# Attention in a hybrid decoder step: turns ahead of both score blocks in each pair's cycle on TensorE

## The chip, the cores and the metric

The kernel runs on one core of one Trainium2 chip. The metric is the device time of one launch in microseconds (us). The engines are PE (TensorE), DVE (VectorE), ACT (ScalarE), POOL (GpSimd) and SP (SyncE, which only issues transfers here). They run their own queues in order and meet through semaphores.

## The reference

Two layers of a decoder over 1024 prompt tokens and 32 sample tokens (8 sequences of 4), width 1024, in float32. What matters here is the attention of both layers:

```
layer 0:  z = rms_norm(x) @ w_in_a
          q, k, v, xq = split(z)              # 12 query heads, 4 kv heads of 64, 4 memory heads
          o  = softmax with sink of (q.k/8 - slope*dist) over a window of 128 keys, times v
          xo = softmax(xq . mem_k) times mem_v  # 256 memory tokens
          x  = x + concat(o, xo) @ w_out_a
layer 1:  the window part is replaced by a chunked spatial gate; the memory attention stays
both:     x  = x + w_down( silu(causal_dwconv3(h w_g)) * (h w_u) ),  h = rms_norm(x)
```

Queries are taken in blocks of 128; a block sees its own keys and those of the block before.

## The kernel before, in words

Every engine's program is written out by hand, and all waits are on counting semaphores. The projections and the feed-forward part are sequences of "units" on TensorE in which each product is formed from three matmuls of high and low parts (lines 613 to 615); they fill most of the time. Between the input projection and the output projection of each layer stands `prompt_attention(l)`, one function per engine (lines 935, 1361 and 1833; the GpSimd part is the loop at line 570).

The attention of the prompt is cut into items, `item_pairs` (line 124). An item is two heads times one block of 128 queries; two neighbouring blocks b and b+1 make a pair. Layer 0 has 32 pairs: numbers 0 to 7 are memory attention, 8 to 31 window attention, four pairs to each of six head tiles. Of those four the first (pairs 8, 12, 16, ...) has b = 0: its even item sees only 128 keys. Layer 1 has 8 memory pairs. An item n goes through these steps:

- **scores** (`scores(n)`, line 941, matmuls at line 959, tiles of 64x64): TensorE writes two PSUM banks, 2*(n%2) and the next. It may not start before the banks' last reader is done: `ready(n-2)` for a window item, `exped(n-2)` for a memory item.
- **top** (`top(n)`, line 1851): DVE takes the row maximum. For a window item this is one instruction per head that also adds the bias and moves the scores to SBUF (line 1871, and a small copy of the sinks at line 1862 for b < 2); for a memory item one reduction (line 1881). It signals `ready`.
- **exps** (line 1366, recorded at line 1382): ACT, two exponentials with row sums; signals `exped`.
- **scale** (line 1883, recorded at 1885): DVE, a reciprocal of the sums; signals `recip`.
- **norm** (`normalise(n)`, line 547, recorded at 553): POOL multiplies both heads; signals `normed`.
- **turn** (`turn(n)`, line 963, recorded at 975): TensorE transposes the probabilities with matmuls against the identity, tiles of 128x128; waits for `normed(n)`.
- **take** (line 1386, recorded at the helper's line 1180): ACT copies the turned block to SBUF (p_t).
- **values** (`values(n)`, line 979, recorded at 994): TensorE multiplies by the values, tiles of 128x64.
- **out** (line 1887, recorded at 1891): DVE copies a pair's result to z.

The pairs are run as a software pipeline. In cycle `it` of the loop TensorE works on the scores of pair it and on the turns and values of pair it-2; DVE does, in this order, scale(2it-2), out(it-3), top(2it), scale(2it-1), top(2it+1) (lines 1946 to 1956); ACT does take, take, then the exponentials of items 2it and 2it+1 (lines 1424 to 1430); POOL normalises item 2it-2 and 2it-1 as their reciprocals arrive. In what follows "even" and "odd" are the first and the second item of a pair.

Between these cycles stand the steps of the sample tokens' attention (`sample_step`, line 800): one in each of ten cycles, from it = 5 on, in layer 0, and four in layer 1. Their matmuls stand at the end of a cycle on TensorE (lines 808, 836, 841, 850, 855, 876, 883 and 887), their scalings in POOL's queue behind the two norms of a cycle (lines 561 and 566), and their copies on DVE at the end of its cycle (line 1801). POOL also makes the window biases in its spare time (line 544) and clears a buffer (line 579) in its queue after the norms of items 2 and 3.

Of the kernel before, what the change touches and what calls it, by code (L numbers as in the profile page):

```python
# [131 lines left out]
def item(layer, n):  # L132

    kind, q, b = item_pairs(layer)[n // 2]
    return kind, q, b + n % 2
# [21 lines left out]
def step_of(steps, layer, it):  # L157

    return steps[layer].get(it - SAMPLE_AT[layer])


def mem_tile(layer, p):
    return (8 if layer == 0 else 12) + p
# [6 lines left out]
def hybrid_step(nc, d, o, slopes):  # L170
    ctx = ExitStack()
    with ctx:
# [432 lines left out]
        def _(pe):  # L605
# [329 lines left out]
            def prompt_attention(l):  # L935
# [3 lines left out]
                M = len(pairs)  # L939

                def scores(n):
                    kind, q, b = item(l, n)
                    if n >= 2:

                        pe.wait_ge(m["ready"] if item(l, n - 2)[0] == "swa" else m["exped"], n - 1)
                    q0 = TS + b * BLOCK
                    for part in range(2):
                        for half in range(2):
                            rows, lanes = slice(64 * half, 64 * half + 64), slice(64 * part, 64 * part + 64)
                            out = ps[lanes, 2 * (n % 2) + half]  # L950
                            if kind == "swa":

                                w0, w1 = max(BLOCK if b == 0 else 0, 64 * part), 192 + 64 * part
                                keys = z[rows, 6 + q // 3, q0 - BLOCK + w0:q0 - BLOCK + w1]
                            else:
                                w0, w1 = 0, 256
                                keys = mem_k[rows, 2 * l + q, :]
                            tile = q if kind == "swa" else mem_tile(l, q)
                            mm = pe.matmul(out[:, w0:w1], z[rows, tile, q0 + 64 * part:q0 + 64 * part + 64], keys,  # L959
                                           start=True, stop=True)  # L960
                    mm.then_inc(m["scored"], 1)

                def turn(n):
                    kind, q, b = item(l, n)
                    pe.wait_ge(m["normed"], n + 1)
                    if n == 0 and l == 0:
                        pe.wait_ge(m["turned_taken"], 5)
                    if n == 0 and l == 1:
                        pe.wait_ge(m["gate_biased"], NB + 1)
                    if n >= 2:  # L970
                        pe.wait_ge(m["pturned_taken"], n - 1)
                    for kc in range(1 if kind == "swa" and b == 0 else 0, 2):
                        for half in range(2):
                            at = (kc * 2 + half) * P
                            mm = pe.transpose(ps[:, 4 + n % 2, at:at + P], se[:, n % RING, half, kc * P:(kc + 1) * P],  # L975
                                              ident[:, :])
                    mm.then_inc(m["pturned"], 1)

                def values(n):
                    kind, q, b = item(l, n)  # L980
                    pe.wait_ge(m["pturned_taken"], n + 1)
                    if n % 2 == 0 and n >= 2:
                        pe.wait_ge(m["o_taken"], n // 2)
                    kc0 = 1 if kind == "swa" and b == 0 else 0
                    for kc in range(kc0, 2):
                        for half in range(2):
                            if kind == "swa":
                                g = 2 * (q // 3) + half
                                vals = v_tok[:, b - 1 + kc, g * HD:(g + 1) * HD]
                            else:  # L990
                                vals = mem_v[:, l, kc, (2 * q + half) * HD:(2 * q + half + 1) * HD]
                            at = (kc * 2 + half) * P
                            o0 = (n % 2) * P
                            mm = pe.matmul(ps[64 * half:64 * half + 64, 6, o0:o0 + P], vals, pt[:, n % 2, at:at + P],  # L994
                                           start=(kc == kc0), stop=(kc == 1))
                    if n % 2 == 1:
                        mm.then_inc(m["pv"], 1)
# [27 lines left out]
                    gate(lambda: scores(0))  # L1025
                    pe.wait_ge(m["gate_biased"], NB)
                for it in range(0 if l == 1 else 2, M + 2):
                    if it < M and (l == 0 or it > 0):
                        scores(2 * it)
                    if it >= 2:  # L1030
                        turn(2 * (it - 2))
                        turn(2 * (it - 2) + 1)
                    if it < M:
                        scores(2 * it + 1)
                    if it >= 2:
                        values(2 * (it - 2))
                        values(2 * (it - 2) + 1)
                    if l == 0 and it == 2:

                        pe.wait_ge(m["z_normed"], 30)  # L1040
                        for t in range(2):
                            mm = pe.transpose(ps[0:TS, 7, t * P:(t + 1) * P], z[:, 6 + t, 0:TS], ident[:, :])
                        mm.then_inc(m["turned"], 1)
                    sample_step(l, step_of(PE_STEPS, l, it))

            for l in range(2):
# [34 lines left out]
                else:  # L1081
                    first_units(2 * l, s0, r0 // 2)
                    for u in range(2, nu):
# [14 lines left out]
                        if u == len(tiles) + 1:  # L1098
                            mixer_stats(l, m, 2, False, True)
                prompt_attention(l)  # L1100

                s0, r0 = (S_OUTA, R_OUTA) if l == 0 else (S_OUTB, R_OUTB)
# [1230 lines left out]
```

## Time and profile before

| | us |
|---|---|
| median of 3 runs | 2269.54 (2268.39 to 2270.66) |
| the profiled execution, its time | 2269.62 |
| its span | 2267.9 |
| PE busy | 2242.6 (99%) |
| DVE busy | 1129.0 (50%) |
| ACT busy | 662.8 (29%) |
| POOL busy | 552.4 (24%) |
| attention of layer 0, first scores to first product of the output projection | 205.2 to 329.9 |
| attention of layer 1 after its gate, second cycle to the end | 1382 to 1412 |

PE works almost all of the time in the projections and the feed-forward part. The stretch that the change touches is the 125 us of layer 0's attention and the last 30 us of layer 1's. In them a row of the timeline is a start in us, a duration, the engine, the line, the operation, its output and inputs, and in brackets the idle time before it and what ended that. The row of a block of matmuls lasts until the modelled end of the last one, so the next block may start before it ends.

### The profile page before, as it was taken

Reading aid. Unit: us, or ns where it says so; the run is one execution under the profiler, and the core shown is the slowest. Engines: PE = TensorE matmul, PEld = TensorE weight load, DVE = VectorE, ACT = ScalarE, POOL = GpSimd, SP = SyncE. Lnnn points to the kernel's source line nnn. Section 1 sums busy time; section 2 is a strip of 40 time slices with the busy share of each in tenths; the row PEclk is TensorE's granted clock in tenths of the full one; section 3 lists DMA queues with packets and bytes.
Section 4 is the critical chain, followed back from the end, with each engine's and each line's share of the span. In section 5 each row is a group of like instructions: output and inputs, shape, how many; then the busy total and the mean of one; then the engine's idle time right before and its main releaser. Section 6 shows DMA issues by size and latency. Waiting matters only on the chain.

```text
span 2267.9 us, 38768 instructions
## 1 busy us (share of the span) xinstructions
PE 2242.6 (99%) x15074; PEld 2149.9 (95%) x15074; DVE 1129.0 (50%) x2142; ACT 662.8 (29%) x1200; POOL 552.4 (24%) x412
## 2 busy tenths in 40 slices
PE   8999999999999999999999999999999999999999
PEld 7987679999999999999999996999999999999999
DVE  6335681565454554454562236246454555454554
ACT  6313791422211222211253226242221122211121
POOL 0002454322211222211261222332221122211221
PEclk9999999999999999999999999999999999999999
DMA  5223001111111111111111111111110111110112
GB/s 171 84 101 136 21 5 47 38 56 56 46 37 37 46 55 55 37 37 45 47 51 51 47 67 67 38 47 57 56 37 29 54 46 55 51 41 28 46 56 90
DMA packets 39303, 123.39 MB, mean 54 GB/s; under 512 B 5328, under 2 KB 13488, under 8 KB 38416
## 3 DMA queue, kind: packets, MB, share of 16 engines
q1 hardware_dynamic: 36384, 113.25, 15.4%
q10 hardware_dynamic: 2832, 8.94, 1.0%
q8 instruction: 60, 0.98, 0.2%
q14 instruction: 27, 0.22, 0.0%
HBM read 115.57 MB, written 8.63 MB: 55 GB/s over the span
## 4 chain that ended last, share of the span: by engine, by line
PE 94%; DVE 3%; ACT 1%; issue 1%; POOL 0%; DMA 0%; SPq 0%; ACTq 0%; DVEq 0%; POOLq 0%
PE ps L613 29%; PE ps L614 28%; PE ps L615 28%; DVE h_lo L1655 2%; PE ps L959 1%; PE ps L994 1%; PE ps L975 1%; PE ps L808 1%; PE ps L928 1%; ACT s_exp L1382 1%; PE ps L777 0%; PE ps L796 0%; PE ps L931 0%; DMA x<-in_x_t 0%; PE ps L907 0%
## 5 line engine op out<-in xcount | busy, mean ns | idle before, releaser
L613 PE MATMUL ps<-h_hi,w_hi 128*128 128x352 f32 x3120 | 1013.7, 325 | 10.6 <-DVE h_lo L1655 10.0
L614 PE MATMUL ps<-h_lo,w_hi 128*128 128x352 f32 x3120 | 1001.3, 321 | 0.0
L615 PE MATMUL ps<-h_hi,w_lo 128*128 128x352 f32 x3120 | 1000.9, 321 | 0.0
L481 POOL TENSOR_TENSOR w_lo<-raw,w_hi 128x1024 fp32r<-128x1024 f32 x118 | 299.2, 2536 | 1518.2 <-ACT w_hi L1180 1518.2
L613 PEld LDWEIGHTS ps<-h_hi,w_hi 128*128 128x128 f32 x3120 | 586.1, 188 | 31.3 <-issue 20.2
L614 PEld LDWEIGHTS ps<-h_lo,w_hi 128*128 128x128 f32 x3120 | 587.4, 188 | 0.0
L615 PEld LDWEIGHTS ps<-h_hi,w_lo 128*128 128x128 f32 x3120 | 585.8, 188 | 0.0
L2055 DVE TENSOR_TENSOR x<-x,ps 128x352 f32<-128x352 f32 x528 | 270.7, 520 | 170.5 <-PE ps L615 169.7
L613 PE MATMUL ps<-g_hi,d_hi 128*128 128x352 f32 x1056 | 340.2, 322 | 0.0
L614 PE MATMUL ps<-g_lo,d_hi 128*128 128x352 f32 x1056 | 339.9, 322 | 0.0
L615 PE MATMUL ps<-g_hi,d_lo 128*128 128x352 f32 x1056 | 339.7, 322 | 0.0
L1180 ACT ACTIVATE w_hi<-raw 128x1024 fp32r<-128x1024 f32 (+1 forms) x140 | 145.3, 1040 | 417.0 <-PE ps L615 403.2
L615 PEld LDWEIGHTS ps<-g_hi,d_lo 128*128 128x128 f32 x1056 | 198.7, 188 | 0.0
L614 PEld LDWEIGHTS ps<-g_lo,d_hi 128*128 128x128 f32 x1056 | 198.4, 188 | 0.0
L613 PEld LDWEIGHTS ps<-g_hi,d_hi 128*128 128x128 f32 x1056 | 198.3, 188 | 0.0
L1180 ACT ACTIVATE g_hi<-g_f 128x352 fp32r<-128x352 f32 x132 | 64.1, 498 | 443.6 <-DVE g_f L2042 443.6
L1981 DVE SCALAR_TENSOR_TENSOR c_buf<-a_buf,conv_c,c_buf 128x1024 f32<-128x1024 f32 x88 | 152.4, 1732 | 2.8
L2028 DVE TENSOR_TENSOR a_buf<-ps,rb 128x352 f32<-128x352 f32 x88 | 46.0, 524 | 211.3 <-PE ps L615 211.3
L2042 DVE TENSOR_TENSOR g_f<-c_buf,ps 128x352 f32<-128x352 f32 x132 | 66.5, 519 | 165.5 <-PE ps L615 163.3
L1461 ACT ACTIVATE c_buf<-c_buf 128x1056 f32<-128x1056 f32 x44 | 47.5, 1078 | 264.0 <-DVE c_buf L1984 264.0
L2124 DVE TENSOR_TENSOR z<-ps,rb 128x352 f32<-128x352 f32 x72 | 37.4, 524 | 173.1 <-PE ps L615 166.9
L481 POOL TENSOR_TENSOR d_lo<-raw,d_hi 128x1024 fp32r<-128x1024 f32 x44 | 106.3, 2417 | 64.1 <-ACT d_hi L1180 64.1
(196 smaller groups left out, 1687.5 us busy)
## 6 DMA issues: line engine op xcount, KB each, us to landing
raw<-in_w SPq DMA_DIRECT2D x181, 512.0 KB, 3.5
s_mk<-in_s_mk SPq DMA_DIRECT2D x2, 2048.0 KB, 9.1
s_mv<-in_s_mv SPq DMA_DIRECT2D x2, 2048.0 KB, 13.6
out_y<-x ACTq DMA_DIRECT2D x7, 528.0 KB
x<-in_x_t SPq DMA_DIRECT2D x2, 1408.0 KB, 12.5
mem_x<-in_mem_t SPq DMA_DIRECT2D x1, 1024.0 KB, 7.6
s_k<-in_s_k SPq DMA_DIRECT2D x2, 512.0 KB, 4.2
s_v<-in_s_v SPq DMA_DIRECT2D x1, 1024.0 KB, 15.6
```

What stands on the lines that cost most here:

```text
L481: pool.tensor_tensor(lo, raw[:, slot], hi.bitcast(F32), ALU.subtract).then_inc(prepped, 1)
L613: pe.matmul(out, a, hi_x(k), start=(first and n == 0), stop=False)
L614: pe.matmul(out, a, lo_x(k), start=False, stop=False)
L615: ins = pe.matmul(out, b, hi_x(k), start=False, stop=(last and n == len(ks) - 1))
L1180: return act.activation(out, in_, ACT.Copy)
L1461: act.activation(c_buf[:, s], c_buf[:, s], ACT.Silu).then_inc(silued[l], 1)
L1655: STT(out=h_lo[:, k, cs], in0=x[:, k, cs], scalar=gain[:, g_i, k:k + 1], in1=h_hi[:, k, cs].bitcast(F32), op0=ALU.mult, op1=ALU.subtract). ...
L1981: ins = STT(out=cp, in0=ab[:, 48 + j:48 + j + SEQ], scalar=cc[:, j:j + 1], in1=cp, op0=ALU.mult, op1=ALU.add)
L2028: ins = TT(ab[:, at:at + CH], ps[:, c, 0:CH], rb[:, c * CH:(c + 1) * CH], ALU.mult)
L2042: TT(g_f[:, c * CH:(c + 1) * CH], c_buf[:, s, c * CH:(c + 1) * CH], ps[:, 3 + c, 0:CH], ALU.mult).then_inc(freed[1], 1)
L2055: TT(xx, xx, ps[:, down_bank(q, last), 0:CH], ALU.add).then_inc(dn_added, 1)
L2124: TT(z[:, unit_tiles(l)[u], cs], ps[:, 3 * (u % 2) + c, 0:CH], rb[:, cs], ALU.mult) \
```

## The change

In the loop over cycles on TensorE the even item's scores move from ahead of the two turns to behind them. Everything else, on TensorE and on the other engines, stays.

```diff
                 for it in range(0 if l == 1 else 2, M + 2):
-                    if it < M and (l == 0 or it > 0):
-                        scores(2 * it)
                     if it >= 2:
                         turn(2 * (it - 2))
                         turn(2 * (it - 2) + 1)
+                    if it < M and (l == 0 or it > 0):
+                        scores(2 * it)
                     if it < M:
                         scores(2 * it + 1)
                     if it >= 2:
                         values(2 * (it - 2))
                         values(2 * (it - 2) + 1)
```

TensorE's queue in layer 0, where the loop begins: line 1007 is the last transpose of the values before the loop, line 1042 a transpose of the sample keys.

```order
 L959 MATMUL ps<-mem_k,z 64x256 x4
 L1007 MATMUL ps<-ident,z 32x128 x2
-L959 MATMUL ps<-mem_k,z 64x256 x4
 L975 MATMUL ps<-ident,s_exp 128x128 x8
-L959 MATMUL ps<-mem_k,z 64x256 x4
+L959 MATMUL ps<-mem_k,z 64x256 x8
 L994 MATMUL ps<-p_t,mem_v 64x128 x8
 L1042 MATMUL ps<-ident,z 32x128 x2
```

The scores of item 4 stood ahead of the turns of items 0 and 1; now they stand behind them, next to those of item 5.

TensorE's queue in layer 0, cycles 9 to 11, where window items are scored (lines 841 and 850 are sample steps):

```order
 L841 MATMUL ps<-ident,s_p 32x128 x3
-L959 MATMUL ps<-z 64x192 x4
 L975 MATMUL ps<-ident,s_exp 128x128 x6
-L959 MATMUL ps<-z 64x192 x4
+L959 MATMUL ps<-z 64x192 x8
 L994 MATMUL ps<-p_t,v_tok 64x128 x6
 L850 MATMUL ps<-ident,s_p 128x128 x2
-L959 MATMUL ps<-z 64x192 x4
 L975 MATMUL ps<-ident,s_exp 128x128 x8
-L959 MATMUL ps<-z 64x192 x4
+L959 MATMUL ps<-z 64x192 x8
 L994 MATMUL ps<-p_t,v_tok 64x128 x8
```

In every cycle one of the two score blocks has moved past the turns. The queues of DVE, ACT, POOL and SP are the same in both kernels.

## Rows read from the trace of the kernel before

**Rows 1.** Busy time by stretch: length, PE, PEld, DVE, ACT, POOL, granted clock, DMA.

```profile
280.00:330.00 50.00, 48.24 (x631) 33.51 (x628) 38.81 (x182) 49.56 (x167) 31.39 (x71) 1.00 0.01 2
```

**Rows 2.** Timeline, cycle 21, window items, all from one execution.

```profile
291.87 0.56 PE L959 MATMUL ps<-z 64*64 64x192 f32 x8
...
292.36 1.09 PE L975 MATMUL ps<-ident,s_exp 128*128 128x128 f32 x8
...
292.63 0.48 DVE L1871 CUSTOM_DVE_ANT_0 s_raw<-ps,bias,nsink_p 128x256 f32<-128x256 f32 x1
...
293.05 1.09 ACT L1180 ACTIVATE p_t<-ps 128x512 f32<-128x512 f32 x2
...
293.38 0.56 PE L959 MATMUL ps<-z 64*64 64x192 f32 x8
...
293.45 0.16 DVE L1885 RECIPROCAL stat<-stat 128x2 f32<-128x2 f32 x1
293.70 0.93 POOL L553 TENSOR_SCALAR s_exp<-s_exp,stat 128x256 f32<-128x256 f32 x2 [0.62 <-DVE stat L1885]
...
293.87 1.09 PE L994 MATMUL ps<-p_t,v_tok 128*64 128x128 f32 x16
294.02 0.51 ACT L1382 ACTIVATE s_exp<-s_raw,stat 128x257 f32<-128x257 f32 x1
294.14 0.48 DVE L1871 CUSTOM_DVE_ANT_0 s_raw<-ps,bias,nsink_p 128x256 f32<-128x256 f32 x1 [0.54 <-PE ps L959]
...
294.89 0.56 PE L959 MATMUL ps<-z 64*64 64x192 f32 x8
```

**Rows 3.** Timeline, cycle 8: POOL's sample scaling and the turn that waits for it.

```profile
245.16 1.14 POOL L561 TENSOR_SCALAR s_p<-s_p,s_stat 128x160 f32<-128x160 f32 x3
...
246.36 0.55 PE L836 MATMUL ps<-ident,s_p 128*128 128x128 f32 x3 [0.55 <-POOL s_p L561]
```

**Rows 4.** Timeline, cycle 20: scores, top and scale where b = 0.

```profile
288.92 0.45 PE L959 MATMUL ps<-z 64*64 64x64 f32 x8
...
289.96 0.34 DVE L1871 CUSTOM_DVE_ANT_0 s_raw<-ps,bias,nsink_p 128x128 f32<-128x128 f32 x1
...
290.50 0.15 DVE L1885 RECIPROCAL stat<-stat 128x2 f32<-128x2 f32 x1
```

**Rows 5.** Timeline: turns of cycle 17, ACT's take after the last exponentials.

```profile
280.70 1.09 PE L975 MATMUL ps<-ident,s_exp 128*128 128x128 f32 x8
...
325.06 1.06 ACT L1180 ACTIVATE p_t<-ps 128x512 f32<-128x512 f32 x2
```

**Rows 6.** Timeline, DVE in cycle 15: sample outputs, then the tops of both items.

```profile
273.44 1.60 DVE L1801 COPY z<-ps 64x32 f32<-64x32 f32 x8
...
275.62 0.48 DVE L1871 CUSTOM_DVE_ANT_0 s_raw<-ps,bias,nsink_p 128x256 f32<-128x256 f32 x1
...
276.50 0.47 DVE L1871 CUSTOM_DVE_ANT_0 s_raw<-ps,bias,nsink_p 128x256 f32<-128x256 f32 x1
```

**Rows 7.** Timeline, the first cycles of layer 0's loop.

```profile
214.96 0.69 DVE L1881 TENSOR_REDUCE stat<-ps 128x2 f32<-128x512 f32 x1 [0.91 <-PE ps L959]
...
216.72 1.86 POOL L544 TENSOR_SCALAR bias<-nd_p 128x256 f32<-128x256 f32 x4
...
218.64 1.16 POOL L579 MEMSET sp_pad<- 128x1280 f32 x1
...
223.85 1.09 PE L975 MATMUL ps<-ident,s_exp 128*128 128x128 f32 x8
```

**Rows 8.** Timeline, layer 1: two score blocks together, then a memory cycle.

```profile
1382.27 1.09 PE L959 MATMUL ps<-mem_k,z 64*64 64x256 f32 x16
...
1388.13 0.66 PE L959 MATMUL ps<-mem_k,z 64*64 64x256 f32 x8
...
1388.93 0.69 DVE L1881 TENSOR_REDUCE stat<-ps 128x2 f32<-128x512 f32 x1 [0.33 <-PE ps L959]
...
1389.54 0.15 DVE L1885 RECIPROCAL stat<-stat 128x2 f32<-128x2 f32 x1
```

## The prediction

> **What bounds the kernel now.** The page's engine shares come first: PE is busy 99% of the span, but the change touches only the attention, so its own stretch has to be read. The busy time by stretch [rows 1] shows there two full engines: of 50 us PE is busy 48.2 and ACT 49.6, at a granted clock of 1.00. Next comes the timeline of one cycle [rows 2]. On PE the even scores start at 291.87, the turns at 292.36, the odd scores at 293.38, the values at 293.87, the next even scores at 294.89: 0.49 + 1.02 + 0.49 + 1.02 = 3.02 us without a gap. ACT needs as much: two takes in 1.09 less an overlap of 0.1, four exponentials of about 0.5. So PE and ACT are bound together, and what the reader should look for is how much room the chains between them have.
>
> The one that matters goes round through DVE and POOL. All in [rows 2]:
>
> - even scores start to top may start: 0.76 (read at the odd block, 293.38 to 294.14, where DVE had been idle and waited for PE; at 291.87 to 292.63 it is 0.76 too)
> - top to scale of the odd item of the pair before, which stands behind it in DVE's queue: 292.63 to 293.45, 0.82
> - scale to the odd norm on POOL: 293.45 to 293.70, 0.25
> - the norm: 0.93
> - norm to the turn that waits for it: 0.06. A wait of that kind is seen once, at the sample step: POOL ends at 245.16 + 1.14 = 246.30, PE starts at 246.36 [rows 3].
>
> Together 2.82. The turn that needs this norm is the second of the next cycle. Before, it comes 3.02 + 0.49 + 0.51 = 4.02 after the start of the even scores, so the chain has 1.2 us to spare and never shows.
>
> **What the change does to it.** No instruction is added, removed or resized, and no transfer is moved. One score block a cycle moves past the two turns. PE then runs turns, even scores, odd scores, values; the odd scores and the values keep their place. The turns come 0.49 earlier, the even scores 1.02 later. Now the even scores stand right behind the second turn, and the chain closes in a single cycle: even scores, top, scale, norm, second turn, next even scores. With the second turn's 0.51 (half of 1.02) it takes 2.82 + 0.51 = **3.33 us**, against 3.02 of work. PE should stand about 0.3 us ahead of the second turn in each cycle. For a pair with b = 0 top to scale is 289.96 to 290.50, 0.54, and its score block lasts 0.45 instead of 0.56 [rows 4], so I estimate 0.65 from scores to top: 0.65 + 0.54 + 0.25 + 0.93 + 0.06 + 0.51 = 2.94.
>
> *Window cycles without sample steps, 17 to 31.* Before, the second turn of cycle 17 starts at 280.70 + 0.51 = 281.21 and the last exponentials end at 325.06 [rows 5]: 43.85. Behind that point both kernels do the same work in the same order. After, from the second turn of cycle 17 to that of cycle 31 there are 14 rounds, 3 of them with b = 0 (20, 24, 28): 11 x 3.33 + 3 x 2.94 = 45.45. From there to the end of the last exponentials: 0.51 to the scores, 0.76 to top(62), 0.88 to top(63) (the distance of two tops back to back, 275.62 to 276.50 in [rows 6]), 0.92 until that is done and ACT starts, and two exponentials, 1.02: 4.09; the even item's exponentials may push it to 4.19, which I take. Sum 49.64, so +5.8. At the entry I give back 0.5: in cycles 13 to 15 DVE's copies of the sample outputs (1.60 us each time, [rows 6]) set when the tops run, wherever the scores stand, so cycle 17's second turn is about 0.5 earlier against that work. **+5.3**.
>
> *The start of layer 0.* Before, item 4's scores run while PE has nothing else to do, and top(4) starts at 214.96 [rows 7]. After, they wait for both turns, and top(4) starts near 218.65. Behind it on DVE is scale(3), 0.6 later, so norm(3) runs from 219.5 to 220.4. Queued behind norm(3) on POOL are four bias instructions (1.86) and the clearing of a buffer (1.16) [rows 7]: norms 4 and 5 end at about 224.4 and 225.4. Cycle 4's second turn needs the last and starts at 225.46, against 223.85 + 0.51 = 224.36 before, and its even scores are then still to do (0.4). That is 1.5, less 0.16 in each of the next cycles (see below): **+1.3**. Bounds: 0, if the turns at once make up the place, and 2.
>
> *The window turn in cycle 8.* It waits for POOL's sample scaling, which stands behind the odd norm [rows 3]; PE already waits 0.55 there. The odd norm moves back with the even scores, by 1.0 at most, and the cycle's work on PE is 0.13 shorter: **+0.8**, bounds 0.4 and 1.1.
>
> *Cycles that PE's own work fills.* In cycles 9 to 14 a sample step of 0.4 to 3.4 us lies between the values and the next turns. It covers most of the chain (0.31), so these cycles lose nothing. This is the cover for the cost that I put at zero here. Two score blocks side by side are also cheaper than two apart. For memory items two take 1.09 together (1382.27 in [rows 8]) and one alone 0.66; each is overlapped by what follows for 0.07, as the turns are in [rows 2] (listed 1.09, next block after 1.02). So 1.02 stands against 2 x 0.59 = 1.18, 0.16 saved; for window items an estimate of 0.13 from their shorter blocks. It counts only where PE sets the pace: **-0.3**.
>
> *Layer 1, and memory cycles in general.* Scores to top is 1388.13 to 1388.93, 0.80, top to scale 0.61 [rows 8]; with 0.25, 0.93, 0.06 and 0.51 the chain takes 3.16, under the 3.33 of the cycle before and level with the 3.17 after the saving. So memory cycles gain 0.1 to 0.16. Layer 1 has six with both turns and scores, and its first turns move into a wait for ACT. Against that the memory turn of its sample step now stands behind a later odd norm, as in cycle 8. Sum **+0.2**, bounds -1 and +1.
>
> The Trainium skill bears on the side by side blocks. "TensorEngine Tiling (Array Packing)", section "Key Properties", says that changing the tiling mode drains TensorE, and the order now changes modes three times a cycle, not four. The page gives no price. By that rule alone the change is a gain; the trace agrees with its direction by the 0.16 of row 1382.27.
>
> Total: 5.3 + 1.3 + 0.8 - 0.3 + 0.2 = +7.3 on the profiled execution's 2269.62 (its span of 2267.9 and 1.7 around it), 2276.9. That execution is 0.08 above the median of the runs, so I predict **2276.8 us**, 0.32% slower.
>
> **Rivals.**
>
> *PE sets the pace, the chain does not bind (faster).* If a turn's norm is there in time, each cycle is its work alone, and 36 cycles save a mode change: 12 memory x 0.16 + 24 window x 0.13 = 5 us, 2264.6. For it: PE is full in [rows 1], takes can start 0.49 earlier, and the rule above. Against it: it decides where the chain is shorter than 2.9 us, and the rows sum to 3.33. Chance 0.08.
>
> *The chain is shorter than its parts (no change that can be told, up to 0.2%, about what a measurement of this kernel can tell from none).* POOL's ends are rough and the 0.06 rests on one wait. With 3.13 for 3.33 the main term falls by 14 x 0.2 = 2.8, and if the start of layer 0 costs half, the total is +3.9: 2273.5. It decides at a chain of 3.18 or less. Chance 0.20.
>
> *A second chain, through ACT, joins in (slower still).* The odd top comes about 0.4 later, so the odd exponentials, the two takes behind them on ACT, and then the values. Round it: 0.76 + 0.88 + 0.92 + 1.0 for the odd item, 1.05 for the takes, 0.1 to the second values, 0.51 for them and 1.02 for the turns, 6.24 in two cycles, 3.12 each. Alone it is under 3.33. If waits for takes and for the norm alternate, a cycle may take 3.6: 14 x 0.27 = +3.8, 2280.6. Chance 0.12.
>
> *The change doesn't do what it says* can be left out: TensorE's order shows the move in every cycle.
>
> **How the numbers follow.** Forecast 0.60, rivals 0.08, 0.20, 0.12. The threshold of 0.2% is 4.5 us, at 2274.1 and 2265.0. Slower takes the forecast and the last rival, 0.72; same 0.20; faster 0.08. The range runs from 2271.0, below the second rival, to 2281.0, the top of the last; what is left out is the fast rival and the ends.
>
> **What would show it.** In the changed kernel's timeline, cycles 17 to 31 should repeat every 3.3 us (3.0 before), with an idle time of 0.2 to 0.4 on PE ahead of the second turn, released by POOL's norm, line 553, and POOL's norm following a scale that stands behind a top. ACT should be under 95% busy in that stretch. The window turn (line 836) should wait some 0.9 on POOL. Layer 0's attention should end 7 us later and layer 1's should keep its length. It is wrong if cycles keep 3.0 us, if PE waits for ACT's takes ahead of the values instead, or if most of the loss stands in the memory cycles.

## The result, and the profile after

The changed kernel takes 2279.69 us (median of 5 runs, 2278.49 to 2279.77), the kernel before 2268.39 (5 runs on the same chip, 2267.48 to 2270.66). The ratio, which is not the quotient of these two medians (1.0050), is 1.0044, 95% interval 1.0031 to 1.0056: slower. The profiled execution took 2279.77 us with a span of 2278.0, against 2269.62 and 2267.9 before.

The head of the changed kernel's page: each engine's busy time, its share of the span and its instructions.

```profile
PE 2242.9 (98%) x15074; PEld 2153.2 (95%) x15074; DVE 1127.4 (49%) x2142; ACT 663.8 (29%) x1200; POOL 552.5 (24%) x412
```

The page hides the change: PE's share falls by one point. The busy time of the window cycles shows it. The row has the columns of [rows 1], for 40 us of the changed kernel:

```profile
280.00:320.00 40.00, 36.31 (x465) 25.00 (x466) 27.58 (x140) 35.76 (x123) 24.15 (x56) 1.00 0.01 2
```

and the same 40 us of the kernel before:

```profile
280.00:320.00 40.00, 40.00 (x532) 27.30 (x530) 31.88 (x156) 39.77 (x138) 26.75 (x62) 1.00 0.01 2
```

At the same granted clock PE is idle for 3.7 us of 40 and ACT for 4.2, where both had been full. No engine is full any more. That is what a chain looks like in this view.

The timeline of the changed kernel, from the second turn of cycle 19 to the scores of cycle 21 (columns as in [rows 2]; in brackets the idle time before and what ended it; PEld is PE's loading of weights, and its row starts with the block of matmuls that it serves):

```profile
289.89 0.66 PE L975 MATMUL ps<-ident,s_exp 128*128 128x128 f32 x4 [0.40 <-POOL s_exp L553]
...
290.48 0.88 PE L959 MATMUL ps<-z 64*64 64x192 f32 x16
...
291.24 0.48 DVE L1871 CUSTOM_DVE_ANT_0 s_raw<-ps,bias,nsink_p 128x256 f32<-128x256 f32 x1 [0.86 <-POOL s_exp L553]
291.38 0.90 PEld L994 LDWEIGHTS ps<-p_t,v_tok 128*64 128x64 f32 x16 [0.37 <-ACT p_t L1180]
...
292.05 0.16 DVE L1885 RECIPROCAL stat<-stat 128x2 f32<-128x2 f32 x1
...
292.31 0.94 POOL L553 TENSOR_SCALAR s_exp<-s_exp,stat 128x256 f32<-128x256 f32 x2 [1.22 <-DVE stat L1885]
...
292.45 0.66 PE L975 MATMUL ps<-ident,s_exp 128*128 128x128 f32 x4
...
293.30 0.66 PE L975 MATMUL ps<-ident,s_exp 128*128 128x128 f32 x4 [0.19 <-POOL s_exp L553]
...
293.88 0.78 PE L959 MATMUL ps<-z 64*64 64x64 f32 x16
...
294.78 0.90 PEld L994 LDWEIGHTS ps<-p_t,v_tok 128*64 128x64 f32 x16 [0.47 <-ACT p_t L1180]
...
296.87 0.21 PEld L959 LDWEIGHTS ps<-z 64*64 64x64 f32 x8 [0.17 <-issue]
```

Follow the chain down it: even scores 290.48, top 291.24 (0.76), scale 292.05 (0.81), odd norm 292.31 (0.26) for 0.94, second turn 293.30 (0.05), next scores 293.88 (0.58). Round: 3.40. The two turns, one group in [rows 2], have come apart, and the second waits. The next round has b = 0 and ends at 296.87: 2.99. In it the turns of cycle 21 stand together again, at 295.85, and wait for nothing.

The chain that ended last, of the changed kernel from 293 to 304 (start, length, engine and line; pieces under 0.2 us left out):

```profile
293.17 0.84 ACT s_exp L1382 x3
...
294.25 0.49 ACT p_t L1180
294.78 1.14 PE ps L994 x16
295.92 1.02 PE ps L975 x8
296.94 0.53 PE ps L959 x8
...
298.71 0.94 POOL s_exp L553 x2
299.69 0.66 PE ps L975 x4
300.35 0.53 PE ps L959 x8
301.04 0.28 DVE s_raw L1871
301.53 0.40 DVE s_raw L1871
302.11 0.94 POOL s_exp L553 x2
303.10 0.66 PE ps L975 x4
```

From 298.71 on it is norm, second turn, first half of the scores, top, norm: no values, no exponentials. Round the pair with b = 0 it takes another way, through ACT's exponentials and takes, the values and both turns. From the scores at 290.48 to those at 296.87 are 6.39 us; the ring just followed would take 3.40 and then about 2.97 (0.61 + 0.55 + 0.25 + 0.93 up to the end of the norm at 296.22, and 0.05 + 0.58 as in the round before), 0.02 less. So the two ways are equally long there. The waits of the changed kernel's layer 0 attention, 200 to 340 (total, times, longest):

```profile
PEld ps L975 <- POOL s_exp L553: 13.0, 22, 2.1
...
ACT s_exp L1382 <- DVE stat L1871: 10.1, 19, 1.1
```

of the kernel before, 200 to 330:

```profile
ACT s_exp L1382 <- DVE stat L1871: 2.1, 2, 1.2
PEld ps L975 <- POOL s_exp L553: 2.0, 3, 1.4
```

The turn's wait for the norm is new in 19 places, and ACT's exponentials wait for DVE in 17 more.

**Where the time went.** The marks are the starts of a line's first matmul in each profile, counted from layer 0's first scores. "Gate" runs in layer 1 from the first matmul of line 907 to the sample step of line 808. It is none of the loop that the change touches.

| stretch | before | after | difference |
|---|---|---|---|
| first scores to the first sample step (L808) | 24.64 | 26.48 | +1.84 |
| to the window turn (L836) | 16.54 | 17.43 | +0.89 |
| to the last sample turn (L883) | 26.39 | 26.52 | +0.13 |
| to the end of the last exponentials | 52.42 | 58.71 | +6.29 |
| to the output projection | 4.71 | 4.72 | +0.01 |
| layer 1, gate | 25.76 | 27.33 | +1.57 |
| layer 1, from L808 to its output projection | 32.27 | 32.33 | +0.06 |

That is 9.2 us in the attention and 1.6 in the gate. The first scores come 0.44 earlier in the second profile and the part behind layer 1's attention is 0.3 shorter; with these the differences make the 10.1 between the spans.

The start and cycle 8 can be read too. On DVE and POOL of the changed kernel, top(4) in the loop's first cycle, norm(3) and what is queued behind it:

```profile
218.35 0.69 DVE L1881 TENSOR_REDUCE stat<-ps 128x2 f32<-128x512 f32 x1 [4.52 <-PE ps L959]
...
219.21 1.16 POOL L553 TENSOR_SCALAR s_exp<-s_exp,stat 128x256 f32<-128x256 f32 x2 [4.35 <-DVE stat L1885]
220.34 1.85 POOL L544 TENSOR_SCALAR bias<-nd_p 128x256 f32<-128x256 f32 x4
222.25 1.16 POOL L579 MEMSET sp_pad<- 128x1280 f32 x1
```

and the two turns of cycle 4, which wait for norms 4 and 5, on PE:

```profile
224.45 0.66 PE L975 MATMUL ps<-ident,s_exp 128*128 128x128 f32 x4 [1.32 <-POOL s_exp L553]
225.35 0.66 PE L975 MATMUL ps<-ident,s_exp 128*128 128x128 f32 x4 [0.25 <-POOL s_exp L553]
```

Before, the top came at 214.96 [rows 7]; now DVE stands idle for 4.52 us ahead of it. In cycle 8 the sample scaling starts at 247.46, not 245.16 [rows 3], right behind an odd norm, and line 836 waits 1.16 where it had waited 0.55:

```profile
247.46 1.14 POOL L561 TENSOR_SCALAR s_p<-s_p,s_stat 128x160 f32<-128x160 f32 x3
...
248.65 0.55 PE L836 MATMUL ps<-ident,s_p 128*128 128x128 f32 x3 [1.16 <-POOL s_p L561]
```

### The profile page after: what moved, and what is told of

Its sections match the earlier page's. It is cut to its first block, busy times and chain, and to the rows that moved or that the text cites. A ratio compares the mean times of both kernels' runs of the same rounds, so it can differ in the third digit from the quotient of the medians.

```text
span 2278.0 us, 38768 instructions
## 1 busy us (share of the span) xinstructions
PE 2242.9 (98%) x15074; PEld 2153.2 (95%) x15074; DVE 1127.4 (49%) x2142; ACT 663.8 (29%) x1200; POOL 552.5 (24%) x412
## 4 chain that ended last, share of the span: by engine, by line
PE 92%; DVE 3%; issue 2%; ACT 1%; POOL 1%; DMA 0%; SPq 0%; DVEq 0%; ACTq 0%; POOLq 0%
PE ps L613 29%; PE ps L614 28%; PE ps L615 28%; DVE h_lo L1655 2%; PE ps L975 1%; PE ps L959 1%; PE ps L994 1%; POOL s_exp L553 1%; DVE s_raw L1871 1%; PE ps L808 1%; ACT s_exp L1382 1%; PE ps L928 1%; PE ps L777 0%; PE ps L796 0%; PE ps L931 0%
```

## The experiments

**Theory A**, the forecast: the loss in the window cycles is the ring of even scores, top, scale, odd norm and second turn. **Theory B**: it is the ring through ACT (tops, exponentials, takes, values), as the takes' waits ahead of the values might suggest. **Theory C**: it has nothing to do with rings, and PE pays for the order by itself. The start and cycle 8 are put down to their own queues. Below are the stretches of each profile in the order of the table above; the clock is that granted in the first 20 us of layer 0's attention and of the gate.

| kernel | to L808 | to L836 | L883 to end of exps | gate | layer 1 | clocks |
|---|---|---|---|---|---|---|
| before | 24.64 | 16.54 | 52.42 | 25.76 | 32.27 | 0.83, 1.00 |
| after | 26.48 | 17.43 | 58.71 | 27.33 | 32.33 | 0.83, 0.91 |
| e1_scale_first | 25.39 | 16.55 | 57.09 | 25.76 | 31.13 | 0.83, 1.00 |
| e2_before_scale_first | 24.27 | 16.27 | 55.85 | 25.76 | 32.28 | 0.91, 1.00 |
| e3_between | 26.65 | 17.16 | 54.43 | 25.76 | 32.50 | 0.74, 1.00 |
| e4_layer1_only | 23.99 | 16.55 | 52.44 | 27.33 | 32.34 | 1.00, 0.91 |
| e5_first_cycle_old | 23.64 | 17.45 | 58.76 | 28.79 | 32.34 | 0.91, 0.83 |
| e6_two_cycles_old | 23.96 | 16.84 | 58.75 | 27.28 | 32.34 | 0.91, 0.91 |
| e7_late_cycles_only | 24.64 | 16.53 | 58.69 | 27.27 | 32.28 | 0.91, 0.91 |
| e8_layer1_both | 24.25 | 16.56 | 52.42 | 25.76 | 31.14 | 0.91, 1.00 |
| e9_after_long_norm | 26.31 | 17.44 | 66.28 | 25.76 | 32.31 | 0.74, 1.00 |
| e10_before_long_norm | 24.63 | 16.55 | 52.55 | 25.76 | 32.29 | 0.91, 1.00 |
| e11_change_again | 26.45 | 17.45 | 58.74 | 25.76 | 32.33 | 0.83, 1.00 |
| e12_memory_cycles | 23.57 | 16.53 | 52.43 | 27.33 | 31.14 | 0.91, 0.91 |

Stretches that run at full clock repeat to 0.1 us in kernels that are alike there. Differences that the medians can't tell can be read from them; the first column can't be read to better than some 0.4.

### e1_scale_first: the scale ahead of the even top

On DVE, with the changed order on PE:

```diff
-                    if it < M and (l == 0 or it > 0):
-                        top(2 * it)
                     if 1 <= it <= M:
                         scale(2 * it - 1)
                     if it < M and (l == 0 or it > 0):
+                        top(2 * it)
+                    if it < M and (l == 0 or it > 0):
                         top(2 * it + 1)
```

The odd norm then no longer depends on the even scores, and theory A's ring is open.

> The change, and on VectorE the odd item's reciprocal put ahead of the even top in each cycle. Theory (the chain even scores, top, odd scale, norm, second turn closes in one cycle): the odd norm no longer stands behind the even top, so PE's idle time ahead of the second turn goes; the next chain, odd exponentials, scale, two tops, odd exponentials, comes to about 3.0 us, so window cycles fall from 3.40 to 3.0 or 3.1 and the time to 2271 to 2274. Rival (later odd exponentials and takes on ScalarE hold the values): nothing is gained, 2279 or more, and window cycles stay at 3.3 or more.

Measured: 2271.59 us, ratio to before 1.0014 (1.0005 to 1.0023). The timeline of this kernel over one window cycle:

```profile
287.06 0.88 PE L959 MATMUL ps<-z 64*64 64x192 f32 x16
...
287.74 1.05 ACT L1180 ACTIVATE p_t<-ps 128x512 f32<-128x512 f32 x2
287.87 0.17 DVE L1885 RECIPROCAL stat<-stat 128x2 f32<-128x2 f32 x1 [0.50 <-ACT s_exp L1382]
288.02 0.48 DVE L1871 CUSTOM_DVE_ANT_0 s_raw<-ps,bias,nsink_p 128x256 f32<-128x256 f32 x1
...
288.37 1.14 PE L994 MATMUL ps<-p_t,v_tok 128*64 128x128 f32 x16 [0.43 <-ACT p_t L1180]
...
288.95 0.51 ACT L1382 ACTIVATE s_exp<-s_raw,stat 128x257 f32<-128x257 f32 x1 [0.15 <-DVE stat L1871]
...
289.44 1.09 PE L975 MATMUL ps<-ident,s_exp 128*128 128x128 f32 x8
...
290.46 0.77 PE L959 MATMUL ps<-z 64*64 64x64 f32 x16
...
291.06 0.17 DVE L1885 RECIPROCAL stat<-stat 128x2 f32<-128x2 f32 x1 [0.50 <-ACT s_exp L1382]
```

The two turns are one group of 8 again and wait for nothing: A's ring is gone. But the cycle is not back at 3.02, nor at the 3.0 or 3.1 that was expected. On PE the one shown takes 3.40 (287.06 to 290.46), and any four in a row, one of them with b = 0, take 12.79, 3.20 each, where the changed kernel has 13.20. A new ring has closed: the scale waits for the odd exponentials, and now both tops wait behind it. Scale 287.87, even top 288.02, even exponentials 288.95, the last of the four over at about 291.04, next scale 291.06: 3.19 in all. It is not the only one. In e2 below, where it stands alone, four cycles take 12.47. In e1 the chain that ended last runs from 284 to 300 through takes, values, turns, scores, tops and exponentials, which is theory B's ring, and the values wait for takes in three cycles of four (0.43 above). How the two share the 12.79 no run separates. The window stretch gains only 1.6 of 6.3; the rest of the drop lies in the start, cycle 8, layer 1 and the gate.

Layer 1 becomes 1.1 shorter than in any kernel so far. The larger part is one wait of the changed kernel, for a POOL scaling that stands behind the odd norm, which e1 doesn't have:

```profile
1402.20 0.44 PE L850 MATMUL ps<-ident,s_p 128*128 128x128 f32 x2 [0.98 <-POOL s_p L566]
```

Its memory cycles without a sample step take 3.07, and 3.23 in the changed kernel (scores at 1411.67 and 1414.90), where A's ring sets them too: 0.80 + 0.61 + 0.25 + 0.94 + 0.05 + 0.58.

### e2_before_scale_first: the same swap in the old order

The control, the DVE edit of e1 on the kernel before.

> The kernel before with the same edit on VectorE alone, as a control for the run above. Both theories: no gain, as the chain has over 1 us to spare there; the even top now waits for the odd exponentials, which may cost 0 to 3 us: 2268 to 2272.

Measured: 2270.80 us, ratio 1.0012 (1.0003 to 1.0021); window stretch +3.4, layer 1 unchanged. The swap is no free way to cut a ring: the scale comes every 3.19 here too (2.89 with b = 0), so it makes the other ring by itself, in either order on PE. It also shows that e1's 1.1 us in layer 1 need both edits.

### e3_between: the even scores between the two turns

```diff
                         turn(2 * (it - 2))
-                        turn(2 * (it - 2) + 1)
                     if it < M and (l == 0 or it > 0):
                         scores(2 * it)
+                    if it >= 2:
+                        turn(2 * (it - 2) + 1)
```

Here the even scores stand ahead of the turn that waits, and they are not in the ring.

> The even scores between the two turns, half of the change. Theory: the second turn no longer stands ahead of the even scores, so the chain does not close in one cycle and window cycles keep 3.0 to 3.15 us, the rest being one more change of tile mode per cycle; about half of the loss at the start of layer 0 stays: 2269 to 2273. Rival (any later even top delays ScalarE's takes and so the values): half of the loss, 2273 to 2275, with PE idle ahead of the values.

Measured: 2272.64 us, ratio 1.0020 (1.0010 to 1.0029). PE in this kernel, one cycle and its end:

```profile
287.56 0.66 PE L975 MATMUL ps<-ident,s_exp 128*128 128x128 f32 x4
288.15 0.56 PE L959 MATMUL ps<-z 64*64 64x192 f32 x8
288.63 0.65 PE L975 MATMUL ps<-ident,s_exp 128*128 128x128 f32 x4
289.22 0.56 PE L959 MATMUL ps<-z 64*64 64x192 f32 x8
289.71 1.09 PE L994 MATMUL ps<-p_t,v_tok 128*64 128x128 f32 x16
290.73 0.66 PE L975 MATMUL ps<-ident,s_exp 128*128 128x128 f32 x4
```

No wait anywhere: 0.59 + 0.48 + 0.59 + 0.49 + 1.02 = 3.17. PE is busy 39.83 of the 40 us from 280 on, so PE is the bound again. A turn that stands alone takes 0.59 where half of a pair takes 0.51, and 14 cycles by 0.15 are the 2.0 that the window stretch grows by. This is theory C's mechanism with its size, 2 us for one more change of block; in the change as made, with one change of block fewer than before and PE idle for 3.7 of 40 us, it can't be the loss. The ring's part is gone with the scores off it. How much of the start's loss stays can't be read: the 26.65 to L808 was taken at a clock of 0.74.

### e9_after_long_norm and e10_before_long_norm: a longer norm

```diff
+                    cuts = [w0, 128, 256] if l == 0 and n % 2 == 1 and n >= 17 else [w0, 256]
                     for half in range(2):
-                        v = se[:, n % RING, half, w0:256]
-                        ins = pool.tensor_scalar(v, v, st[:, n % 4, 2, half:half + 1], 1.0, ALU.mult, ALU.mult)
+                        for c0, c1 in zip(cuts, cuts[1:]):
+                            v = se[:, n % RING, half, c0:c1]
+                            ins = pool.tensor_scalar(v, v, st[:, n % 4, 2, half:half + 1], 1.0, ALU.mult, ALU.mult)
```

From item 17 on the odd norm is done in four pieces of 128 columns in place of two of 256: the same result, a longer time on POOL, which has room (24.15 busy of 40). e9 has it with the changed order, e10 with the old one. If the ring sets the pace, e9 must pay the whole length each cycle, and e10 nothing.

> The change, and the odd window items' norm on GpSimd cut into four pieces of 128 columns for two of 256, from pair 8 on: 4 x 0.37 for 0.93 us, 0.55 more per cycle by the rows of 128-column norms. Theory (the norm lies in the chain that sets the cycle): the 17 cycles without sample steps grow by 0.4 to 0.55 each, and some with them, so 7 to 11 us on top of the changed kernel: 2286 to 2291. Rival (GpSimd is not in the limiting chain): 2279 to 2281.

> The kernel before with the same longer norm. Theory: the chain has 1.2 us to spare there, so 0.55 more is hidden: 2268 to 2270. Rival (the norm is already near the path before): 2273 or more.

Measured: e9 2287.59 us, ratio 1.0078 (1.0062 to 1.0093); e10 2269.69, ratio 0.9999 (0.9990 to 1.0008). The window stretch grows by 7.57 over the changed kernel's in e9 and by 0.13 over that of before in e10. The cycle of e9 that answers to the one shown above (the added lines move every line number behind them by 2; the norm's row joins the four pieces of the odd norm, about 1.4, and the two instructions of the next even one):

```profile
292.22 0.88 PE L961 MATMUL ps<-z 64*64 64x192 f32 x16
...
294.05 2.35 POOL L555 TENSOR_SCALAR s_exp<-s_exp,stat 128x128 f32<-128x128 f32 x6 [1.56 <-DVE stat L1887]
...
295.51 0.66 PE L977 MATMUL ps<-ident,s_exp 128*128 128x128 f32 x4 [0.80 <-POOL s_exp L555]
296.10 0.77 PE L961 MATMUL ps<-z 64*64 64x64 f32 x16
```

The round is 3.88, 0.48 more than 3.40. All of it is the norm: from its start to the turn that waits for it are 1.46 (294.05 to 295.51) where the changed kernel has 0.99 (292.31 to 293.30), and the other steps of the ring are as they were. One for one: this is the run that settles A. In the ring through ACT the odd norm has no place; by B alone e9 would have cost nothing until the norm had used up a slack. The round with b = 0 grows as much, from 2.99 to 3.46 (296.10 to 299.56). And the 1.2 us of room that the prediction gave the old order swallowed the same 0.48 there.

### e7_late_cycles_only: the new order from cycle 17 on

```diff
+                    late = l == 0 and it >= 17
+                    if not late and it < M and (l == 0 or it > 0):
+                        scores(2 * it)
                     if it >= 2:
...
-                    if it < M and (l == 0 or it > 0):
+                    if late and it < M and (l == 0 or it > 0):
                         scores(2 * it)
```

> The changed order only in layer 0's cycles 17 to 31 and the last two. Theory: the whole loss of the window cycles without sample steps, and nothing of the start or of the window turn: 6 to 7 us over the kernel before, 2274.5 to 2275.5. Rival (the loss is made up at the start and carried): under 3 us.

Measured: 2275.97 us, ratio 1.0026 (1.0015 to 1.0037). That is 0.5 above what was expected. The window stretch has its whole +6.27, everything ahead of it is as before. The window cycles alone are thus over two thirds of the loss. The next kernels have the same edit with another condition for `late`.

### e5_first_cycle_old and e6_two_cycles_old

`late = l == 1 or it != 2` in e5, `late = l == 1 or it not in (2, 8)` in e6: the new order everywhere but in the first cycle of layer 0's loop, or in the first and cycle 8.

> The change everywhere but in layer 0's first cycle (it = 2), which keeps the old order. In the changed kernel's profile the window scores of the sample step come 1.8 us later after the first scores than before. Theory: that comes from item 4's scores standing behind both turns, with POOL's queue of norm, biases and clearing behind them: 1.5 to 2 us less than the changed kernel, 2277 to 2278.5 where that gives 2279.5. Rival (it is the later memory cycles): no gain.

> As the run before, and the old order in cycle 8 too, whose sample turn waits for a scaling behind the odd norm on GpSimd. Theory: 0.7 to 1 us less again, 2276 to 2277.5, and the wait of the turn at line 836 back at 0.6 us from 1.2. Rival (that wait was hidden in what follows): no further gain.

Measured: e5 2276.85 us, ratio 1.0036 (1.0022 to 1.0049), 1.0 under e11, the changed kernel on the same chip; e6 2274.98, ratio 1.0027 (1.0017 to 1.0037). With one cycle back in the old order the first sample step comes 2.8 earlier than in the changed kernel (23.64 for 26.48; a part of it is the clock, 0.91 for 0.83). Kernels with the old order all through the start, at that clock, have 24.25 to 24.64 (e2, e7, e8, e10), those with it in the first cycle and the new one behind it 23.64 and 23.96 (e5, e6). So the start's loss sits in that single cycle, and the new order in cycles 3 to 7 is a small gain. In e6 the wait at line 836 is back at 0.56, and the stretch to it is 16.84, 0.6 less than 17.43 and 0.3 more than with the old order throughout: cycle 8's loss is mostly its own, and where the other 0.3 lies no run separates.

### e4_layer1_only, e8_layer1_both, e12_memory_cycles

`late = l == 1` in e4. e8 adds the scale ahead of the even top, in layer 1 alone:

```diff
+                    if l == 1 and 1 <= it <= M:
+                        scale(2 * it - 1)
                     if it < M and (l == 0 or it > 0):
                         top(2 * it)
-                    if 1 <= it <= M:
+                    if l == 0 and 1 <= it <= M:
                         scale(2 * it - 1)
```

e12 is e8 with `late = l == 1 or it in (3, 4, 5)`, the memory cycles of layer 0 after its first. It is put together from what gained in the other runs.

> The change in layer 1 alone. Theory: its memory cycles gain and lose about nothing, within 0.5 us; if the granted clock falls in the spatial gate, as in the profile of the changed kernel, 1.5 us more: 2268 to 2270.5. Rival (memory cycles lose as window cycles do, 0.3 us each): 2271 or more, with idle time ahead of the turns there.

> Candidate: layer 0 as before; in layer 1 the changed order on TensorE and, on VectorE, the odd scale ahead of the even top. In the first run's profile that part took 31.1 us where the kernel before took 32.3. Theory: memory cycles save a change of tile mode once the chain is opened: 1 us faster than before, 2267.3. Rival (that was chance in one execution): same as before, 2268.4.

> Candidate: as the layer 1 candidate, and the changed order in layer 0's cycles 3, 4 and 5 alone (memory pairs ahead of the first sample step); all other cycles of layer 0 as before. Theory: where the chain through GpSimd has room, each cycle saves a change of tile mode, 0.16 us, and in layer 0 some of the wait for ScalarE: about 1.1 us in layer 1, 0.3 to 0.8 in layer 0; 1.4 to 1.9 us faster than before. Rival (the gain in layer 0 was the clock of one execution): 1.1 us as with layer 1 alone. Medians of a kernel move by up to 1.5 us from call to call, so the stretches in the profile decide, not the median.

Measured: e4 2268.39 us, ratio 0.9999 (0.9990 to 1.0008); e8 2267.50, ratio 0.9994 (0.9985 to 1.0003); e12 2268.45, ratio 0.9995 (0.9986 to 1.0004). The stretches show in e4 nothing (+0.07 in layer 1), in e8 1.13 less in layer 1, where four memory cycles save 1.0 together (3.07 for 3.33 where no sample step stands in one), in e12 the same 1.13 and a further 0.7 to the first sample step at e8's clock. Two us in all are less than the medians can tell from none: neither kernel is shown to beat the one before.

### e11_change_again: the changed kernel once more

> The changed kernel once more, on the chip of the two runs above, for their comparison and for the clock: in its first profile the granted clock fell to 0.69 in 5 us of layer 1's spatial gate, which the change does not touch, and cost 1.5 us; it stayed at 1.00 in the profile of before. If that comes and goes from execution to execution, this one may show it or not, and the time lies between 2278 and 2280; if it belongs to the changed kernel, it is there again.

Measured: 2277.86 us (5 runs, 2277.70 to 2278.96), ratio 1.0041 (1.0027 to 1.0055). Every stretch of the attention repeats to 0.03 us, but the gate takes 25.76, as before. The rows of the gate, busy time by stretch with the granted clock third from the end, first of the changed kernel's first profile, then of this one:

```profile
1368.80:1373.80 5.00, 5.00 (x31) 3.86 (x31) 1.92 (x2) 0.81 (x1) 0.00 (x0) 0.69 1.02 416
```

```profile
1368.00:1373.00 5.00, 5.00 (x44) 4.00 (x44) 2.86 (x3) 1.27 (x3) 0.27 (x1) 1.00 1.03 423
```

PE is busy throughout in both; at a clock of 0.69 it does 31 matmuls where it does 44 at 1.00. e4 keeps the old order in all of layer 0, and has the fall too (27.33); e1, e3, e9 and e11, with other orders, have not. So the 1.57 us are an event of an execution and not of the change.

## Why the prediction was right, and where its sizes were off

| step | predicted | measured |
|---|---|---|
| window cycles 17 to 31 | +5.3 | +6.3 |
| start of layer 0 | +1.3 (0 to 2) | +1.8 |
| window turn, cycle 8 | +0.8 (0.4 to 1.1) | +0.9 |
| cycles that PE fills | -0.3 | +0.1 |
| layer 1's loop | +0.2 (-1 to +1) | +0.1 |
| gate, not in the sum | | +1.6, by the execution |

The forecast was 2276.8, the measurements are 2279.7 and 2277.9, both inside the range, and the mechanism is the forecast one: theory A, shown by e9 and e10, with e3 for the scores' place in the ring. The size was too small: +7.3 was forecast, and the profiled executions differ by 10.1, or by 8.5 without the gate.

- **The chain's parts** were right to 0.01 each, read from a kernel in which it never showed: 0.76, 0.81, 0.26, 0.94, 0.05 for 0.76, 0.82, 0.25, 0.93, 0.06, sum 2.82. The rival of a shorter chain is out.
- **The second turn, taken as 0.51 (half of 1.02), is the term that was mis-sized.** 0.51 is its share when it runs on behind the first. Once it waits, it stands alone, and the next block starts 0.58 after it (293.30 to 293.88 above). The round is 3.40, not 3.33, and 2.99 with b = 0, not 2.94: 11 x 0.07 + 3 x 0.05 = 0.9 of the missing 1.0. With b = 0 the two rings tie: a lone second turn would give 2.97, but the turns stand together there, and the 2.99 are 0.90 from the scores to the values, which wait for ACT's takes, 1.07 for the values and 1.02 for the turns. From the second turn of cycle 17 to that of 31 the changed kernel takes 46.3 for the forecast 45.45 and from there to the end of the last exponentials 4.4 for 4.19, while the 0.5 given back at the entry came out as 0.5 (4.4 + 46.3 - 43.85 - 6.3). The trace of before shows such a group of four nowhere; half of a group of eight was a lower bound only, and e3's 0.59 has the same size with no wait at all, so it is the lone turn's own cost.
- **The start** was right in its steps, 0.5 short in its sum. Everything in the changed profile is 0.44 early, as its first scores are. With that added norm(3) starts at 219.65 (forecast 219.5) and takes 1.16 (forecast 0.93), and cycle 4's second turn starts at 225.79 (forecast 225.46): 0.3 of the missing 0.5.
- **Cycle 8** and **layer 1** came out as reckoned. For layer 1 the two entries that were set against each other are both there. The cycle of line 850 grows from 3.60 to 4.39, most of it the 0.98 of waiting shown at e1, and three of its neighbours shrink by 0.8 together: from the second turn group of the loop to the sixth both kernels take 15.63. Of the sums behind it, the memory ring takes 3.23 for the forecast 3.16, the lone turn again, and PE's own work 3.07 for 3.17. e4 shows that with DVE's order as it is the new order is worth nothing, e8 that with the scale ahead it is worth 1.1.
- **The cycles that PE fills** lost 0.1 where 0.3 was to come back. A saving exists in memory cycles (e5, e6 and e12 at the start). In cycles 10 and 11 the changed profile has waits that the one of before lacks, 0.26 for a norm ahead of a second turn and 0.17 and 0.29 for takes ahead of values: a short sample step doesn't cover the chain, which the prediction had put at nothing there. How much of them stays in the time no run separates.
- **The rival through ACT** joins in weakly. The loading of the values' weights ends its wait with a take (0.37 and 0.47 above), and the values start 0.90 after the even scores where 0.81 is the scores' own time. In a round of 3.40 this is made up before the second turn, which waits the less for it (0.19 above); the round is the other ring's sum, and e9's one for one leaves this one no share. Around a cycle with b = 0 it is as long as the other ring, 6.39 in two cycles where the prediction had 6.24. So it stands close behind.
- **PE sets the pace** would have made this a gain. The saving is real where PE is the bound: the memory cycles of layer 1 in e8 take 3.07 where the old order takes 3.33, 0.1 of which is a wait ahead of the even scores; and the opposite case costs 0.15 a cycle in e3. The ring costs 0.38 a window cycle (3.40 for 3.02). The Trainium skill ("TensorEngine Tiling (Array Packing)", "Key Properties") says that a change of the tiling mode drains TensorE; e8 and e3 agree with its direction, and the rule says nothing of the ring.
- **The gate's** 1.6 us was in no term, and it isn't the change's. Of the distance between 2276.8 and the first measurement's 2279.7 it makes 1.6, and the attention's 9.2 for the forecast 7.3 makes 1.9; the earlier start and the shorter end give 0.7 back.

One thing is left open: all five runs of the first measurement lie above 2278.4, and three of the five of the second at 2277.9 or below. The gate can explain such a difference in one execution, but the profile shows only one execution of each.

## What to carry to other kernels

Before an instruction is moved on an in-order engine, follow what leaves it round the other engines until it comes back, through those instructions too that merely stand behind another in a queue, and set the sum of one round against the cycle. As long as the way back enters behind the moved instruction there is a cycle of room; once it enters ahead of it, each round costs the sum less the cycle, with all engines part idle. Price a block that will wait by itself as one that stands alone, not by its share of a group. And when a ring is cut by another swap, look for the ring that the swap closes (e1, e2) and for the next longest one before counting on the whole gain.

## What the hardware showed that had not been expected

- A group of four 128x128 turns between other blocks takes 0.58 to 0.59 to the start of the next block, half of a group of eight 0.51. Window score blocks take 0.81 side by side (in a cycle of e1 without a wait, 293.66 to 294.47) and 2 x 0.49 apart [rows 2], more than the 0.13 that was estimated as their saving.
- The granted clock falls in the gate for some microseconds in 6 of 14 profiles, with PE busy all the while, and the gate then takes 27.3 or 28.8 for 25.76 (0.91 and 0.83 over its first 20 us). In layer 0's first 20 us it is between 0.74 and 1.00 in these profiles, whatever the order.
- The norm cut in 128-column pieces costs 0.37 a piece, 256 columns 0.48: half the columns save a quarter.
